# A mixer block with 32 experts on one core: order of the first loads, place of branch B's decay work, layout of the expert weight loads

## The reference, cut to what matters

```python
z = x @ w_in                                   # 256 x 1024 @ 1024 x 11016: columns for A, B, C, D and the gates
# branch B (hgrn2_mix), 4 heads of 128 channels; the lower bound lb is 0 here (one layer)
q, f, i, g = split(zB, (512,) * 4)
q = silu(q); log_f = log_sigmoid(f); k = sigmoid(-f)
b = cumsum(log_f)                              # per channel, over tokens
o[t] = sum over s <= t of (q[t] . (k[s] * exp(b[t] - b[s]))) * i[s]
yB = head_rmsnorm(o) * norm_w * silu(g)
...
x = layernorm(ALPHA * x + (sum over n of gate_n * (y_n @ w_branch[n])) @ w_out)
# experts: 32, the best 4 for each token
gu = xb @ w_gu[e] + b_gu[e]                    # 1024 -> 2048
gate, up = min(gu[:, :1024], 7), clip(gu[:, 1024:], -7, 7)
y = ((up + 1) * gate * sigmoid(1.702 * gate)) @ w_down[e] + b_down[e]
```

## Time and profile before

| | |
|---|---|
| time before, median of 3 runs | 1976.13 us (1975.95 to 1977.58) |
| the profiled execution's own time | 1977.81 us |
| its span in the trace | 1975.7 us |
| mean granted TensorE clock | 0.976 |
| TensorE busy | 1834.2 us, 93% |
| queue of SyncE's loads | 527.53 MB, 68.1% of 16 DMA engines' span |

### The profile page before, as it was taken

One profiled execution on the slowest core, in us unless ns is written; L12 is line 12 of the kernel. 1 busy time (PEld: TensorE's weight loads), 2 busy tenths in 40 slices (PEclk: granted clock), 3 DMA queues, 4 the chain that ended last, 5 costly groups with the idle time before them and its releaser, 6 DMA issues. The chain is left out here.

```text
span 1975.7 us, 21417 instructions
## 1 busy us (share of the span) xinstructions
PE 1834.2 (93%) x8829; PEld 1066.4 (54%) x8829; DVE 553.8 (28%) x1037; ACT 235.7 (12%) x379; POOL 43.9 (2%) x39
## 2 busy tenths in 40 slices
PE   6999999799999999988989989989889879999998
PEld 5787887599864334333333333333333326768984
DVE  0643487555244311110111111101101121014412
ACT  0322112100100001110100101101101111011100
POOL 1000000121000000000000000000000000000000
PEclk9999999799898999999999999999999998999999
DMA  7333333521138999999999999999999976542331
GB/s 254 128 128 128 129 107 107 191 86 61 70 123 295 370 408 418 419 417 418 418 416 420 417 416 419 417 418 418 417 419 418 417 300 222 158 140 86 102 129 63
DMA packets 134058, 537.69 MB, mean 272 GB/s; under 512 B 5746, under 2 KB 13212, under 8 KB 101112
## 3 DMA queue, kind: packets, MB, share of 16 engines
q1 hardware_dynamic: 128880, 527.53, 68.1%
q10 hardware_dynamic: 3464, 4.85, 0.9%
q0 software_dynamic: 1664, 4.58, 0.8%
HBM read 531.18 MB, written 5.77 MB: 272 GB/s over the span
## 5 line engine op out<-in xcount | busy, mean ns | idle before, releaser
L1164 PE MATMUL small<-arena 128*64 128x512 f32 x2048 | 459.3, 596 | 67.1 <-DMA arena<-in_expert_w_gu 67.1
L1164 PEld LDWEIGHTS small<-arena 128*64 128x64 f32 x2048 | 157.9, 137 | 362.3 <-issue 233.4
L622 PE MATMUL proj<-arena 128*128 128x256 f32 x992 | 224.2, 388 | 8.7 <-DMA arena<-in_w_in_first 6.3
L1196 PE MATMUL small<-arena 128*64 128x512 f32 x1024 | 226.8, 594 | 5.8 <-issue 5.8
L2102 DVE TENSOR_SCALAR arena<-small 128x512 f32<-128x512 f32 x32 | 22.1, 691 | 742.1 <-PE small L1171 742.1
L622 PEld LDWEIGHTS proj<-arena 128*128 128x128 f32 x992 | 192.8, 196 | 37.2 <-issue 10.4
L1217 PE MATMUL proj<-arena 128*128 128x256 f32 x768 | 167.5, 379 | 0.0
L1217 PEld LDWEIGHTS proj<-arena 128*128 128x128 f32 x768 | 145.4, 190 | 20.3 <-issue 1.0
L1196 PEld LDWEIGHTS small<-arena 128*64 128x64 f32 x1024 | 84.7, 137 | 127.4 <-issue 127.4
L1335 ACT ACTIVATE arena<-proj 128x512 f32<-128x512 f32 (+1 forms) x76 | 44.9, 597 | 533.7 <-PE proj L873 169.6
L1470 ACT ACTIVATE arena<-arena 128x512 f32<-128x512 f32 x32 | 20.1, 630 | 570.0 <-DVE arena L2102 570.0
(11 more groups left out here) (443 smaller groups left out, 1603.3 us busy)
## 6 DMA issues: line engine op xcount, KB each, us to landing
arena<-in_expert_w_gu SPq DMA_DIRECT2D x128, 2048.0 KB, 24.5
arena<-in_expert_w_down SPq DMA_DIRECT2D x64, 2048.0 KB, 21.4
arena<-in_w_in_first SPq DMA_DIRECT2D x21, 2048.0 KB, 7.8
arena<-in_w_in SPq DMA_DIRECT2D x16, 2048.0 KB, 9.1
arena<-in_w_ada SPq DMA_DIRECT2D x6, 2048.0 KB, 8.0
arena<-in_w_branch SPq DMA_DIRECT2D x4, 2048.0 KB, 8.2
arena<-in_w_out SPq DMA_DIRECT2D x4, 2048.0 KB, 8.0
bias_rows<-arena ACTq DMA_DIRECT2D x1, 4608.0 KB
```

Of the source, the lines that this page charges most:

```text
L622: mm = pe.matmul(ps[:, m * T:m * T + T], w[:, k, (2 * b + m) * P:(2 * b + m + 1) * P], XT[:, k, :], start=k == 0, stop=k == KD - 1)
L1164: mm = pe.matmul(bank[CAP * half:CAP * half + CAP, :], XG[:, k % 4, k // 4, :], w[:, k % 2, n * D + half * W:n * D + half * W + W], start= ...
L1196: mm = pe.matmul(y_bank[CAP * half:CAP * half + CAP, :], HM[:, m, u, :], w[:, m, half * W:half * W + W], start=u == 0 and m == 0, stop=u = ...
```

## The change

1. The load of unit "D xr" is issued in two halves of 256 columns, with a semaphore of its own for the first. TensorE does bank 0 of "D xr" when the first half is in, then turns the vectors, and then does bank 1.
2. The constants are issued after the third unit ("C q") in place of the first.
3. Branch B's f is projected before its q. ScalarE's and VectorE's steps for the running sum (absolute value, Exp, Ln, subtraction, scans, `differences(0)` and its exponential) come earlier: VectorE does them between the weights of branch C and the copies of branch C's products, and f lies in another buffer (`fB0`, which is `tB2`).
4. Expert weights: partition p takes rows 2p and 2p + 1 of a w_gu unit and rows 4p to 4p + 3 of a w_down unit, which are 16 KB in one run. The turns of `XR` and `GH` read their columns in steps of 2 and 4 floats to match.

```diff
-UNITS = ([... "C o", "B q", "B f", "B i", "B g",
+UNITS = ([... "C o", "B f", "B q", "B i", "B g",
...
+        fB0 = tB2
...
             if u < 4:
                 src = ins["expert_w_gu"][0, bass.ds(e, 1), u * 2 * P:(u + 1) * 2 * P, :]
-                return src.rearrange("e (k p) n -> p (e k) n", p=P), (2, GU)
+                return src.rearrange("e (p k) n -> p (e k) n", p=P), (2, GU)
             src = ins["expert_w_down"][0, bass.ds(e, 1), (u - 4) * 4 * P:(u - 3) * 4 * P, :]
-            return src.rearrange("e (k p) n -> p (e k) n", p=P), (4, D)
+            return src.rearrange("e (p k) n -> p (e k) n", p=P), (4, D)
...
                 src, _ = unit_source(name)
+                if n == 0:
+                    sp.dma_start(weights(name)[:, :, 0:T], src[:, :, 0:T]).then_inc(sig("first_half"), 16)
+                    sp.dma_start(weights(name)[:, :, T:W], src[:, :, T:W]).then_inc(sig("unit_in_0"), 16)
+                    continue
                 sp.dma_start(weights(name), src).then_inc(sig(f"unit_in_{n % 3}"), 16)
-                if n == 0:
+                if n == 2:
                     sp.dma_start(CO[:, P:], consts["consts"][:, P:]).then_inc(sig("const_loaded"), 16)
...
-            ones_channels("D xr")
-            ones_channels("D gate")
+            pe.wait_ge(sig("first_half"), 16)
+            w = weights("D xr")
+            ps = proj("D xr 0")
+            for m in range(2):
+                for k in range(KD):
+                    mm = pe.matmul(ps[:, m * T:m * T + T], w[:, k, m * P:m * P + P], XT[:, k, :], start=k == 0, stop=k == KD - 1)
+            mm.then_inc(sig("proj_full"), 1)
             pe.wait_ge(sig("prow_loaded"), 16 * len(VEC))
             pe.transpose(small("vectors")[:, 0:NVEC], PROW[0:NVEC, :], ident[0:NVEC, 0:NVEC]).then_inc(sig("small_full"), 1)
+            ones_channels("D xr", (1,))
+            ones_channels("D gate")
             ones_channels("C q")
...
-            ones_channels("B q")
+            ones_channels("B f")
             pe.wait_ge(sig("const_loaded"), 16)
...
-            ones_channels("B f")
+            ones_channels("B q")
...
-                    mm = pe.transpose(bank[:, m * P:m * P + P], XR[:, m * P:m * P + P], ident)
+                    mm = pe.transpose(bank[:, m * P:m * P + P], XR.rearrange("s (u p k) -> s u p k", u=2, k=2)[:, m // 2, :, m % 2], ident)
...
-                    mm = pe.transpose(gate_bank[:, m * P:m * P + P], GH[:, m * P:m * P + P], ident)
+                    mm = pe.transpose(gate_bank[:, m * P:m * P + P], GH.rearrange("s (p k) -> s p k", k=4)[:, :, m], ident)
...
-            channels("B q", qB)
+            channels("B f", fB0)
             act.wait_ge(sig("C_dist"), 1)
+            log_and_exp()
             do(act.activation(wC, wC, ACT.Exp, scale=-1.0), "C_w")
...
-            channels("B f", fB)
+            channels("B q", qB)
+            act.wait_ge(sig("B_absf"), 1)
+            do(act.activation(cB, cB, ACT.Exp, scale=-1.0))
+            do(act.activation(cB, cB, ACT.Ln, bias=1.0), "B_ln")
...
             rsqrt(stC[:, 2, :], "C_var", "C_rstd")
-            act.wait_ge(sig("B_absf"), 1)
-            do(act.activation(cB, cB, ACT.Exp, scale=-1.0))
-            do(act.activation(cB, cB, ACT.Ln, bias=1.0), "B_ln")
+            act.wait_ge(sig("B_diff"), 1)
+            act.activation(eBs[0], eBs[0], ACT.Exp).then_inc(sig("B_exp"), 1)
             gates("D", 0)
...
             dve.nop().then_inc(sig("C_weights"), 1)
+
+            dve.wait_ge(sig("proj_out"), proj_no("B f 1") + 1)
+            do(STT(cB, fB0, -1.0, fB0, ALU.mult, ALU.max), "B_absf")
+            dve.wait_ge(sig("B_ln"), 1)
+            do(STT(fB, fB0, 0.0, cB, ALU.min, ALU.subtract))
+            for m in range(KW):
+                do(dve.tensor_tensor_scan(cB[:, m, :], c("ones"), fB[:, m, :], 0.0, ALU.mult, ALU.add))
...
+            differences(0)
             for j in range(TT):
                 do(dve.tensor_copy(hC[:, 4 * j:4 * j + 4, :], tiles(full(f"C num {j}"), P)), "small_out")
...
-            dve.wait_ge(sig("proj_out"), proj_no("B g 1") + 1)
-            do(STT(cB, fB, -1.0, fB, ALU.mult, ALU.max), "B_absf")
             dve.wait_ge(sig("B_sig"), 1)
...
-            dve.wait_ge(sig("B_ln"), 1)
-            do(STT(fB, fB, 0.0, cB, ALU.min, ALU.subtract))
-            for m in range(KW):
-                do(dve.tensor_tensor_scan(cB[:, m, :], c("ones"), fB[:, m, :], 0.0, ALU.mult, ALU.add))
...
-            differences(0)
             merge("D", True)
```

More of the change, by code:

```diff
@@ L108 @@
 NVEC = _place_vectors()
-UNITS = (["D xr", "D gate", "C q", "C k", "C if", "C v", "C o", "B q", "B f", "B i", "B g",
+UNITS = (["D xr", "D gate", "C q", "C k", "C if", "C v", "C o", "B f", "B q", "B i", "B g",
           "G D 0", "G D 1", "Wb D", "A r", "A k", "A v", "A x",
@@ L1402, in _ @@
             do(act.activation(tB, qB, ACT.Sigmoid))
-            do(act.activation(kB, fB, ACT.Sigmoid, scale=-1.0))
+            do(act.activation(kB, fB0, ACT.Sigmoid, scale=-1.0))
             do(act.activation(eB, gB, ACT.Sigmoid), "B_sig")
@@ L1414, in _ @@
             for l in range(9):
-                if l < 8:
+                if 0 < l < 8:
                     act.wait_ge(sig("B_diff"), l + 1)
@@ L1702, in _, with halves, differences @@
             dve.nop().then_inc(sig("C_weights"), 1)
+            dve.wait_ge(sig("proj_out"), proj_no("B f 1") + 1)
[4 more added lines that the diff above has]
+                do(dve.tensor_tensor_scan(cB[:, m, :], c("ones"), fB[:, m, :], 0.0, ALU.mult, ALU.add))
+            def halves(v, l):
+                v = v.rearrange("p a (n r i) -> p (a n) r i", r=2, i=1 << l)
+                return v[:, :, 0, :], v[:, :, 1, :]
+            def differences(l):
+                left, right = halves(cB, l)
+                e_left, e_right = halves(eBs[l % 2], l)
+                ref = left[:, :, (1 << l) - 1:1 << l].to_broadcast([P, 4 * T // (2 << l), 1 << l])
+                if l > 1:
+                    dve.wait_ge(sig("small_full"), small_no(f"B level {l - 2} 1") + 1)
+                do(TTn(e_right, right, ref, ALU.subtract))
+                do(TTn(e_left, ref, left, ALU.subtract), "B_diff")
+            differences(0)
             for j in range(TT):
```

## The result

The changed kernel takes **1945.38 us** (median of 4 runs, 1943.18 to 1947.88) against 1976.04 for the kernel before on the same chip: a ratio of 0.9849 [0.9829, 0.9869], 30.7 us less. A later repeat on another chip gave 1945.01 against 1978.02, 0.9836 [0.9823, 0.985]. The profiled execution took 1947.88 us, with a span of 1945.7 where 1975.7 stood before.

A forecast was written before the change was run, and what follows sets the result against it. The expert loop was taken as bound by its loads, the rest by TensorE. 1977.8 - 23.9 (loop) - 9.0 (start), with 0 for turns and branch B, gave 1944.9, by the median 1943 us; range 1930 to 1962.

The forecast's parts named there:

- What bounds the loop: Expert loop: loads bound it at 30.12 us a step (418 GB/s), with TensorE's own step at 27.16 us.
- The loop's term: Expert loads in 16 KB runs: 29.35 us a step, 0.77 us saved, over 31 steps 23.9 us.
- my line: Packet cost from two DMA windows: 11.4 ns a packet and 37.3 ns a KB, giving 29.2 us a step.
- The turns: Stepped reads in the expert loop: 0 taken, up to 1.15 us more a step, hidden under the loads.
- The start: Kernel start to "C q": first matmul at 11.3 instead of 16.46, end at 56.2 instead of 65.25, 9.0 us saved.
- the slow beginning of 2.7 us: "D xr" and "D gate" at the start: 30.62 us as before, not the 27.96 of the later pace.
- Branch B: Moved forget-block work: 9 us fits into VectorE's 27.81 us wait, but the 3.82 us gap stays; 0 saved.
- The chain named: Before branch B's first level, TensorE waits for D's last merge, diagonal banks, level 1's exponents, level 0's products; none moved.
- A: Rival, expert loads: a partition's rows stay separate packets, steps stay at 30.12 us, 1967 us; chance 0.10.
- B: Rival, expert loads: a packet's fixed cost is a third, 3.8 ns; 0.30 us a step, 1958 us; chance 0.08.
- C: Rival, expert loop: stepped turns become the bound; at four times as long, 30.61 us a step, 1995 us; chance 0.05.
- D: Rival, expert loads: address spacing drops the rate below 414 GB/s; at 381, 33.0 us a step, 2056 us; chance 0.03.

The follow-up runs named there:

- e1: The kernel before with only the 16 KB expert load layout and its stepped turns added: 1953.51 us, ratio 0.9884.
- e3: The kernel before with only branch B's new order on ScalarE and VectorE, old start and expert layout: 1975.60 us, ratio 0.9994.
- e2: The kernel before with only the new start (halved first block, constants two units later, vectors turned early): 1967.91 us, ratio 0.9961.
- e11: The changed kernel run again without any edit: 1945.01 us.
- e10: The changed kernel with level 1's exponents and level 0's products on VectorE moved ahead of D's merge: 1939.24 us, ratio 0.9817 against the kernel before.
- e12: Repeat of e10, the same edit to the changed kernel: 1939.04 us, ratio 0.9802 against the kernel before.

## Why the prediction was right

It said 1943 (1930 to 1962) and the kernel takes 1945.38. By its own steps:

- **What bounds the loop.** Right: the loads, before and after. TensorE's own 27.21 us stayed 2.2 us under the load line.
- **The loop's term**, 0.77 us a step and 23.9 in all. Measured: 0.75 a step, 23.2 by the steps and 22.6 by e1's time. The sum held because I took less than my line gave, for the uncertain edges of a window; so its closeness is in part luck. The line itself had 11.4 ns a packet; the runs have 9.3 to 9.4. I had drawn it through a window of 2 KB packets at 381 GB/s from the start of the kernel, with other loads in flight; what makes it slower than 9.35 ns a packet was not tried. The row with 16.8 KB packets at 431 GB/s was the better guide: the plateau is 429.
- **The turns**, 0, with up to 1.15 us hidden. Right in the sum (0.05 us of TensorE's step, hidden). The rule that was weighed is not what the rows show: the step of 2 pays as much as the step of 4, 67 or 68 ns of a weight load.
- **The start**, 9.0 us. At "C q" it was 9.9 between the two profiled executions: the first matmul at 11.39 (11.3 said), the end at 55.34 (56.2 said). Where I kept the slow beginning of 2.7 us, the 192 matmuls took 44.0 us; I had 30.6 + 14.0 = 44.6. But one step was wrong: I put it down to the wait for ScalarE that "C q" took 15.58 us before and not 13.98, and counted the 1.6 us as saved. e3 has the same wait and took 14.05; the rest was the granted clock, which fell behind the wait in the kernel before (and in e1, 15.71) and not in e3. Without it my sum is 7.4, and against e3 the gain is 7.1. e2's 8.2 us (4.9 to 10.3) does not tell 7.1 from 9.9. The last L1183 comes 7.2 us before e1's in the changed kernel's first profile (1581.63 - 1574.43) and 9.3 in e11 (1572.29), which is the same code. So no run shows that a part is lost on the way, as the difference lies within one kernel's executions. The windows of 560 to 700 us show where some of it arises (columns as above); the kernel before:

```profile
560.00:700.00 140.00, 135.57 (x504) 66.06 (x505) 46.83 (x99) 7.85 (x15) 4.78 (x8) 0.95 0.77 280
```

And the changed kernel:

```profile
560.00:700.00 140.00, 135.64 (x492) 62.45 (x492) 43.90 (x95) 7.88 (x15) 4.78 (x8) 0.93 0.82 302
```

  TensorE was as busy, but at 0.93 instead of 0.95 of full clock. 2% of 135 us is 2.7 us, about the 2.5 by which the gain shrank between branch B's first level (9.92) and the first L1183 (682.91 - 675.50 = 7.41). In e11 the same window has 0.95 again, and the first L1183 comes at 673.49, 9.4 us earlier than before. That points to the clock of one execution and not to a cost of the change.
- **Branch B**, 0. Measured 0.6 us, inside the uncertainty. The chain named was the right one: e3 keeps the gap, and e10 and e12, which cut just that chain, take it away and gain 6.0 us. My bound of -5 for the case that the level could start at once was 1 us short, as it did not count all that the clock behind the gap gives back.
- **Rivals.** A (rows stay separate packets) falls by the packet count, 785 where it needed some 2040. B (a packet costs 3.8 ns) falls by the table: 9.3 to 9.4. The rule that it was set beside, of the Trainium skill, DMA: Bandwidth & Descriptors, Why small descriptors are slow, has about 3 cycles for a packet, and beside them 32 bytes of metadata, one cycle more. With a cycle of 32 bytes at this loop's 435.1 / 16 GB/s, 1.18 ns, that is an estimate of 3.5 to 4.7 ns by the page, about half of what these steps show, or less. C (the turns as the bound) needed them 3.8 times as long; the matmuls went from 286 to 308 and from 273 to 285 ns. D (a rate under 414 GB/s) falls by 429 GB/s.

## What to carry to other kernels

In a loop bound by its loads, count packets: here each cost about 9.35 ns of an engine beside its bytes, so that letting a partition take neighbouring rows (16 KB instead of 4 and 8) gave 2.5% of a step for two access patterns and a hidden stride in the turns. Moving work earlier wins only if it is on the chain that the waiting engine follows: the forget block's move gave nothing until the last two products of the chain were moved too, and then 6.0 us. Before a difference between two profiles is booked to a change, look at the granted clock in the same window of other executions: here 1.5 us of "C q" were the clock's. At a kernel's start the first matmul needs half a block, and the first small operation of another engine (here the turned vectors) can be what holds the third block back.

## What the runs showed of the hardware that was not expected

- Large loads from HBM go at 429 GB/s on this one core and, carried on to no packets, at 435.1 (an estimate), and the fixed cost of a packet is the same 9.3 to 9.4 ns whether the packets that are split are of 16 into 8 or into 4 KB.
- A weight load of 128x128 floats read in steps of 2 takes 208 ns, in steps of 4 209, and 141 close together.
- The same gap of 3.82 us before the first level of branch B is followed by a lower granted clock in most executions and not in all: the 16 + 32 matmuls behind it took 2.05 + 7.07 us in the changed kernel (1.00 from 220 to 240 us), 2.46 + 8.38 in e11, which is the same code (0.91), and 2.58 + 8.26 in the kernel before (0.91). In e12, without a gap, they took 1.95 + 7.07 (1.00). The wait of 2.47 us before "C q" is the same: 15.58 us behind it in the kernel before (0.86), 14.05 in e3 (1.00). What decides whether the clock falls stays open.
